# Moving the small attention matmuls of a two-block forward pass between slots, and giving the norm's column and the head weights whole tiles

## The reference

```python
proj = xn @ w_in                                  # qa ka va qb kb vb qi ki wi xc yc gates
dots = jnp.einsum('bqhd,bsd->bqhs', qiq, ki)      # indexer: 8 heads of 64
score = jnp.einsum('bqh,bqhs->bqs', wq, jax.nn.relu(dots)) * idx_scale
_, idx = lax.top_k(score, n_keep)                 # 64 keys are kept
...
p = jax.nn.softmax(logits, axis=-1)               # 16 heads of 64, as 8 pairs
out = einsum(p, v)
y = x + (sum over branches of g * (y_branch @ w_p)) @ w_o
```

## Time and profile before

| what | us |
|---|---|
| median of 3 runs | 772.01 (771.97 to 772.43) |
| the profiled execution | 772.69 |
| its span, first to last instruction | 770.9 |
| PE busy | 748.0 (97%) |
| DVE busy | 556.7 (72%) |
| ACT busy | 393.7 (51%) |

### The profile page before, as it was taken

How to read it: one execution, slowest core, us unless ns; L and a number is a source line. 1 busy time by engine, 2 the same in 40 slices (tenths; PEclk the granted TensorE clock), 3 DMA queues, 4 the chain that set the end, 5 groups by cost and what they waited for, 6 DMA issues and landing times. The chain is left out here.

```text
span 770.9 us, 13469 instructions
## 1 busy us (share of the span) xinstructions
PE 748.0 (97%) x5568; PEld 706.7 (92%) x5568; DVE 556.7 (72%) x879; ACT 393.7 (51%) x476; POOL 175.8 (23%) x109
## 2 busy tenths in 40 slices
PE   5999999999999998999999999999999999999996
PEld 5999999999999998999999899999999888888885
DVE  5396966999875786878898866566876755655564
ACT  6544545466562547653755455554347544354443
POOL 4898797971000010600013110000000000000000
PEclk9999999999999999999999999999999999999998
DMA  9866554546626587473554645535645465456521
GB/s 320 276 194 200 175 173 124 186 142 192 212 88 207 192 286 233 130 258 120 165 164 137 202 154 178 178 111 190 219 128 200 165 218 185 165 195 216 178 96 54
DMA packets 117384, 138.91 MB, mean 180 GB/s; under 512 B 4657, under 2 KB 107857, under 8 KB 117202
## 3 DMA queue, kind: packets, MB, share of 16 engines
q1 hardware_dynamic: 116706, 136.50, 54.9%
q0 software_dynamic: 480, 1.57, 0.8%
q10 hardware_dynamic: 144, 0.06, 0.0%
HBM read 133.93 MB, written 4.19 MB: 179 GB/s over the span
## 5 line engine op out<-in xcount | busy, mean ns | idle before, releaser
L507 ACT ACTIVATE s_whi<-s_raw 128x2048 fp32r<-128x2048 f32 (+1 forms) x93 | 174.2, 1875 | 52.0 <-PE sums L1460 28.4
L848 DVE TENSOR_TENSOR s_wlo<-s_raw,s_whi 128x2048 fp32r<-128x2048 f32 (+2 forms) x68 | 151.1, 2225 | 61.6 <-ACT s_whi L507 61.4
L1458 PE MATMUL sums<-s_a_parts,s_whi 128*128 128x256 f32 x576 | 163.5, 284 | 2.0 <-DVE s_wlo L848 2.0
L1459 PE MATMUL sums<-s_a_parts,s_whi 128*128 128x256 f32 x576 | 163.0, 283 | 0.0
L1460 PE MATMUL sums<-s_a_parts,s_wlo 128*128 128x256 f32 x576 | 163.0, 283 | 0.0
L1458 PE MATMUL sums<-s_b_hi,s_whi 128*128 128x256 f32 (+1 forms) x536 | 154.0, 287 | 0.8 <-DVE s_reg_d L1013 0.8
L1459 PE MATMUL sums<-s_b_lo,s_whi 128*128 128x256 f32 (+1 forms) x536 | 151.6, 283 | 0.0
L1460 PE MATMUL sums<-s_b_hi,s_wlo 128*128 128x256 f32 (+1 forms) x536 | 151.6, 283 | 0.0
L431 POOL TENSOR_TENSOR s_wlo<-s_raw,s_whi 128x1024 fp32r<-128x1024 f32 x52 | 128.2, 2494 | 28.0 <-ACT s_whi L507 27.8
L1458 PEld LDWEIGHTS sums<-s_a_parts,s_whi 128*128 128x128 f32 x576 | 110.6, 192 | 2.7 <-DVE s_wlo L848 2.2
L1459 PEld LDWEIGHTS sums<-s_a_parts,s_whi 128*128 128x128 f32 x576 | 110.6, 192 | 0.0
(11 more groups left out here) (310 smaller groups left out, 1297.7 us busy)
## 6 DMA issues: line engine op xcount, KB each, us to landing
s_raw<-in_w_in SPq DMA_DIRECT2D x61, 1024.0 KB, 5.7
s_raw<-in_w_up SPq DMA_DIRECT2D x16, 1024.0 KB, 5.5
s_raw<-in_w_down SPq DMA_DIRECT2D x16, 1024.0 KB, 6.8
s_raw<-in_w_pa SPq DMA_DIRECT2D x6, 1024.0 KB, 5.1
s_raw<-in_w_pb SPq DMA_DIRECT2D x6, 1024.0 KB, 5.5
s_raw<-in_w_out SPq DMA_DIRECT2D x4, 1024.0 KB, 5.2
s_raw<-in_w_ple_gate SPq DMA_DIRECT2D x4, 1024.0 KB, 7.4
s_raw<-in_w_o SPq DMA_DIRECT2D x4, 1024.0 KB, 5.7
```

The lines of the kernel that those rows point to most:

```text
L507: act.activation(ring_view(whi, c), ring_view(raw, c), ACT.Copy).then_inc(Sm["hi_ready"], 1)
L848: ve.tensor_tensor(dst, src, part.bitcast(F32), ALU.subtract).then_inc(Sm["lo_ready"], 1)
L1458: pe.matmul(dst, sh, mh, start=first and k == 0, stop=False)
L1459: pe.matmul(dst, sh, ml, start=False, stop=False)
```

## The change

`values` leaves the odd slots. It runs one unit later, ahead of the next pair's `probs_T` and of the `scores` of the pair behind it: behind unit 64+2t now come `values(t-2)`, `probs_T(t-1)` and `scores(t)`. ACT's `round_o` and DVE's `lo_o` move back by one pair with it, and the last pair's `values` runs behind unit 82. `dots` of pairs 0 and 1 both run behind unit 54 and those of pairs 2 and 3 both behind unit 56; the wait for wi_ready goes. r_col is made with a stationary tile of all 128 partitions of r_bc and one column of o128 (each entry 1/128), and wi is taken out of full 128*128 transposes of r3_bc; both go to M[4].

```diff
--- before.py
+++ after.py
@@ -744,12 +744,14 @@
                     if 0 <= t < PAIRS:
                         exps(2 * t)
                         exps(2 * t + 1)
-                elif 1 <= t <= PAIRS:
-                    round_o(t - 1)
+                elif 2 <= t <= PAIRS:
+                    round_o(t - 2)
 
             for j in range(6):
                 if j < 4:
                     hi(FIRST["pc2"] + 3 + j)
+                if j == 1:
+                    round_o(PAIRS - 1)
                 if j >= 4:
                     for half in range(2):
                         n = 2 * (j - 4) + half
@@ -1213,10 +1215,10 @@
                     else:
                         ve.wait_ge(Sm["rcol_T"], 1)
                         ve.wait_ge(Sm["wi_T"], 1)
-                        ve.tensor_copy(r_col[:, :], M[3][:, 0:NR]).then_inc(Sm["rcol_ready"], 1)
+                        ve.tensor_copy(r_col[:, :], M[4][:, S:S + NR]).then_inc(Sm["rcol_ready"], 1)
                         ve.wait_ge(Sm["rcol_ready"], 1)
                         for r in range(NR):
-                            ve.tensor_scalar(wi[:, r, :], M[2][:, HEADS * r:HEADS * (r + 1)], r_col[:, r:r + 1],
+                            ve.tensor_scalar(wi[:, r, :], M[4][:, P * r + DH:P * r + DH + HEADS], r_col[:, r:r + 1],
                                              None, ALU.mult).then_inc(Sm["wi_ready"], 1)
                     drain(d, xc[:, 2 * j:2 * j + 2, TAPS2 - 1:TAPS2 - 1 + S], bc)
                 elif kind == "yc":
@@ -1305,8 +1307,8 @@
                     if t < PAIRS:
                         normalise(2 * t)
                         normalise(2 * t + 1)
-                    if 1 <= t <= PAIRS:
-                        lo_o(t - 1)
+                    if 2 <= t <= PAIRS:
+                        lo_o(t - 2)
 
 
 
@@ -1352,6 +1354,8 @@
                     ve.wait_ge(Sm["vchain"], chain[0])
                     ve.wait_ge(Sm["dve_drained"], drained_count(c))
                 lo(c + 3)
+                if n == 1:
+                    lo_o(PAIRS - 1)
 
             for j in range(4):
                 c = FIRST["wo"] + j
@@ -1718,12 +1722,12 @@
             def attention(c):
                 t, odd = divmod(c - HEAD_AT, 2)
                 if not odd:
+                    if 2 <= t <= PAIRS + 1:
+                        values(t - 2)
                     if 1 <= t <= PAIRS:
                         probs_T(t - 1)
                     if 0 <= t < PAIRS:
                         scores(t)
-                elif 1 <= t <= PAIRS:
-                    values(t - 1)
 
             for c in range(FIRST["ki"], FIRST["pc2"]):
                 kind, j = UNITS[c]
@@ -1738,23 +1742,22 @@
                     columns(c, b_hi, b_lo)
                 if c == FIRST["ki"] + 2:
                     pe.wait_ge(Sm["rb_ready"], 1)
-                    pe.wait_ge(Sm["x2_ready"], 4)
+                    pe.wait_ge(Sm["s2_std"], 1)
                     for r in range(NR):
-                        ins = pe.matmul(M[3][:, r:r + 1], r_bc[0:1, P * r:P * r + P], ones[0:1, 0:1], start=True,
+                        ins = pe.matmul(M[4][:, S + r:S + r + 1], r_bc[:, P * r:P * r + P], o128[:, 0:1], start=True,
                                         stop=True)
                     ins.then_inc(Sm["rcol_T"], 1)
                 if c == FIRST["ki"] + 2:
                     pe.wait_ge(Sm["dve_drained"], drained_count(FIRST["ki"]))
                     for r in range(NR):
-                        ins = pe.transpose(M[2][:, HEADS * r:HEADS * (r + 1)], wiT[:, P * r:P * r + P],
-                                           ident[DH:DH + HEADS, DH:DH + HEADS])
+                        ins = pe.transpose(M[4][:, P * r:P * r + P], r3_bc[:, P * r:P * r + P], ident[:, :])
                     ins.then_inc(Sm["wi_T"], 1)
                 if IDX_AT <= c < IDX_AT + 4:
-                    if c == IDX_AT + 1:
-                        pe.wait_ge(Sm["wi_ready"], NR)
                     if c == IDX_AT:
                         pe.wait_ge(Sm["dve_drained"], drained_count(FIRST["ki"]))
-                    dots(c - IDX_AT)
+                    if (c - IDX_AT) % 2 == 0:
+                        dots(c - IDX_AT)
+                        dots(c - IDX_AT + 1)
                 if c == LRU_AT:
                     pe.wait_ge(Sm["relu_done"], HEADS)
                     pe.wait_ge(Sm["xcc_ready"], 1 + NT * TAPS2)
@@ -1779,8 +1782,8 @@
 
             pe.wait_ge(Sm["yc_lo"], 1)
             branch(FIRST["pc2"], c_hi, c_lo, 0)
-            attention(FIRST["pc2"])
             branch(FIRST["pc2"] + 1, c_hi, c_lo, 0)
+            attention(FIRST["pc2"] + 1)
             pe.wait_ge(Sm["o_lo"], 4)
             branch(FIRST["pb2"], a_hi, a_lo, 0)
             branch(FIRST["pb2"] + 1, a_hi, a_lo, 0)
```

## The result

The changed kernel takes 775.35 us in the median of 20 runs (773.39 to 776.54). Beside it the kernel before took 772.49 us (771.97 to 775.29, 20 runs). The ratio of the two is 1.0027, with a 95% interval of 1.0019 to 1.0036: slower by 2.1 us (1.5 to 2.8), or by 2.9 us as the medians stand. The profiled execution took 774.82 us. The lines of DVE and PE stand 2 to 4 further down than in the kernel before (L1675 is L1679, L1690 is L1694), those of ACT named here (L507, L682, L706) where they were.

The account below looks back on a forecast made before the run. PE, busy 748.0 of 770.9 us, was taken as the bound; +1.85 us (stall, net of both merges) plus 0 (attention), added to the 772.01 us median, gave 773.8 us, range 772.2 to 774.6.

Parts of the forecast that it names:

- The stall: PE before dots(3) behind unit 56: waits some 2.0 us for relu 3, shifting PE by 1.85 us.
- Rival B: PE's waits at 411 and 425 us swallow the 1.85 us shift; not slower, 772.0 us; chance 0.12.
- rival E: Attention seam costs 0.2 us, or the stalled PE comes back slowly: 774.5 us and more; chance 0.04.
- the sum: Whole kernel: +1.85 us for the stall, net of both merges, plus 0 for the attention, giving +1.85 us.
- Attention: Values beside transposes and scores on PE: four seams before and after, 0 us, between -0.7 and +0.7.
- Merged dots: Dots of two pairs together on PE: two pairs of seams removed, 2 x 0.19 = 0.38 us saved.
- Small forms: r_col and wi on full tiles behind unit 54: +0.1 us on PE, between -0.1 and +0.3.
- rival D: Relus 2 and 3 are done before dots(3) asks: 770.9 to 772.3 us, likeliest 771.6; chance 0.05.

Follow-up runs that it names:

- e5: The changed kernel with ACT's relus of an iteration put ahead of the gelu of yc; median 771.28 us, ratio to before 0.9978.
- e4: The changed kernel with 16 spare products between dots(2) and dots(3), where PE sits idle; median 773.86 us, ratio to before 1.0013.
- e8: The changed kernel with 6 spare products between dots(2) and dots(3); median 773.94 us, ratio to before 1.0007.
- e6: The changed kernel with only dots(0) and dots(1) together, dots(2) behind unit 56 and dots(3) behind unit 57 as before; 772.16 us, ratio 0.9995.
- e7: The changed kernel with dots(2) and dots(3) both behind unit 57 instead of unit 56; median 771.34 us, ratio to before 0.9986.
- e3: The kernel before with only r_col and wi made on whole 128*128 tiles in M[4]; median 772.45 us, ratio 0.9991.
- e1: The kernel before with only values moved ahead of the next transposes and scores; median 772.06 us, ratio 0.9987.
- e2: The kernel before with the new r_col and wi and dots merged into two visits, attention as before; median 775.95 us, ratio 1.0032.

## Why the prediction was right, and where it was short

**The stall** was right in place, cause and size. I forecast dots(3) held by relu 3 for some 2.0 us (2.15 measured), ACT's gelu in front of the relus as the reason (e5 takes it away), and a shift of PE of 1.85 us. e4 and e8, which have the stall without the slow products, show 1.75 us. The 0.10 less is a seam: with dots(3) gone from behind unit 57, unit 58 no longer stands behind a small form, and its seam out of it falls away (from its first product to the gate matmuls 5.86 us before; in e4 units 57 and 58 take 11.62 us together, 5.77 us beside unit 57's 5.85). I had let the stall hide all that the second merge saves.

**No absorption.** Rival B wanted the later waits to swallow the shift. DVE's split of unit 62 waited for PE, the 1.5 and 0.6 us waits stayed what they were, and all of it passed through (398.9 and 398.7 us from the first gate matmul to the end).

**The term that was missing** is TensorE's clock behind the stall: 1.50 us, nearly as much as the stall's own 1.75. I had named a slow return of PE as one half of rival E and gave that 0.04. That was the weak step: the sum priced the stall as idle time alone, and put at nothing what came behind it. The two add up to +3.25 us up to unit 58, less 0.2 us in the attention, less the 0.9 us that the profile before had lost ahead of the edits at 302 us: +2.1 us, the difference of the two spans. The medians, 2.86 us apart, lie near 3.25 - 0.2. The median stands 1.5 us above my 773.8, and above the 774.6 at which my range ended: 1.0 us of it is the larger shift, and 0.5 us is that the kernel before came to 772.49 us in 20 runs where I had started from 772.01. By the ratio, 1.0027 on 772.01, the time is 774.1 us and inside the range. So the forecast that the kernel would be slower, and why, held; that the size did is in part luck, since a term of 1.5 us was missing and by the median it was rival E, the one with the slow return, that came true. In the 4 of 20 executions that ended under 774 us (773.39 to 773.83, mean clocks 0.998 and 0.999 where the others have 0.995 to 0.998) the sum of the prediction holds; they weren't profiled, so that these lack the half clock is argued from their time and mean clock.

**Seams.** Attention: I took 0 between -0.7 and +0.7, measured are 7 x 0.03 = 0.2 us gained. The count of four seams and four was right. Merged dots: I took 0.19 us each and 0.38 are measured (e5, e6, e7), because more than the seams to products falls away: behind the last group of the first pair the next row comes after 0.22 us instead of 0.32, and the second pair's own groups stand 0.10 us closer. Small forms: +0.1 us forecast, +0.08 measured (e3).

**No stall**, rival D, gives 771.3 us in e5 and e7, where I had written 771.6. By the distances the gain is 0.9 us where I had 0.4: the merges save twice what I took, and the attention 0.2 us.

What stays open: why the clock fell in most executions and not in some.

## What to carry to other kernels

When small jobs are gathered on one engine, each keeps its own wait; ask for each where the work that releases it stands in the other engine's queue, and move that too (e5), or gather at the later place (e7). Price a stall of TensorE twice, as idle time and as what the clock may cost behind it (1.75 and 1.50 us here), and look first for a place where nothing waits. Putting a small form beside full tiles saved 0.03 us a pair here (e1); putting two visits of one form together saved 0.38 us (e5 to e7).

## What was not expected of the hardware

An idle time of 2.15 us on PE, behind 26 us in which it had waited for nothing, was followed by some 3.4 us at a granted clock of 0.50 (361.2 to 364.6), in which 14 products took 0.21 us each. The Trainium skill, TensorE: Matmul & The Clock Gate, What's actually happening, says that the gate's level follows how busy the array has been; e4 and e8 agree, where the gap was filled or half filled and the clock stayed. The length of an idle time alone doesn't decide it. The 1.5 us before the first scores left the clock at 1.00 in every profile here, and so did 2.0 us at 302 us in the kernel before and 2.4 to 2.6 us there in e2, e3 and e6. But in the profile of e1 the clock fell behind an idle time of 1.8 us at the same place:

```profile
302.85 0.39 PE L1462 MATMUL sums<-s_a_parts,s_whi 128*128 128x256 f32 x1 [1.81 <-DVE s_wlo L850]
```

```profile
303.50:306.50 3.00, 3.00 (x16) 3.00 (x16) 3.00 (x5) 2.35 (x6) 0.00 (x0) 0.50 0.84 259
```

That execution took 773.91 us, where 9 of e1's 12 took 771.57 to 772.66. Such a stretch at a place that no edit touches may be why some executions of the kernel before take 774 to 776 us too; this is not shown, since none of those was profiled.
